# A hybrid RG-LRU and pooling layer on one core: the last norm of a block moved behind the next block's heads, small copies on POOL, split parts first in a head pair

## The reference

```python
proj = rmsnorm(x, norm1_g) @ w_in                  # 1024 -> 4096: x_a | x_b | g_a | g_b
c = causal_conv4(x_a)                              # state: last 3 rows
r, i = sigmoid(c @ w_r + b_r), sigmoid(c @ w_i + b_i)   # 8 heads of 128
a = exp(8 * r * log_sigmoid(lam)); bt = sqrt(1 - a*a) * i * c   # 1 for the root at position 0
h[t] = a[t] * h[t-1] + bt[t]                       # scan over time
d = moving_mean(x_b, windows 2, 4, 8, 16) - x_b    # state: last 15 rows
y_b = grouped(d @ pool_w) * pool_scale
merged = sigmoid(g_a) * (h @ w_br_a) + sigmoid(g_b) * (y_b @ w_br_b)
x = x + merged @ w_out
x = x + (silu(n @ w_g) * (n @ w_u)) @ w_down       # n = rmsnorm(x, norm2_g), hidden 2816
y = rmsnorm(x, final_g)
```

## Time and profile before

| | |
|---|---|
| time, median of 3 runs | 2940.25 us (2940.04 to 2941.14) |
| the profiled execution, its own time | 2941.63 us |
| its span, first to last instruction | 2939.8 us |
| TensorE busy | 2874.5 us (98%) |
| VectorE, ScalarE busy | 1956.4 us (67%), 1263.1 us (43%) |
| POOL busy | 0.2 us, 4 instructions |
| granted clock of TensorE, mean | 0.990 |
| DMA | 354.43 MB, 121 GB/s |

### The profile page before, as it was taken

The page is one execution under the profiler, slowest core; times in us unless marked ns, Lnnn a source line. Parts: engine busy times, 40 slices in busy tenths (PEclk is TensorE's granted clock), DMA queues, the critical chain, the costliest instruction groups (busy, mean ns, idle before and its releaser), DMA issues.

```text
span 2939.8 us, 37519 instructions
## 1 busy us (share of the span) xinstructions
PE 2874.5 (98%) x15006; PEld 2829.8 (96%) x15006; DVE 1956.4 (67%) x2946; ACT 1263.1 (43%) x1745; POOL 0.2 (0%) x4
## 2 busy tenths in 40 slices
PE   8799999999999999999999999999999999999998
PEld 7789999999999999999999999999999999999998
DVE  7657666667576676776666757766667576666656
ACT  4743433347434333483333325833333366343222
POOL 0000000000000000000000000000000000000000
PEclk9999999999999999999999999999999999999999
DMA  4263333333334333333333333334333333333332
GB/s 142 83 219 110 137 122 115 115 108 124 130 118 142 115 108 122 107 117 130 129 130 109 122 115 117 129 115 138 115 115 117 120 110 122 111 107 127 115 117 81
DMA packets 113163, 354.43 MB, mean 121 GB/s; under 512 B 12128, under 2 KB 30816, under 8 KB 112992
## 3 DMA queue, kind: packets, MB, share of 16 engines
q1 hardware_dynamic: 102480, 336.14, 33.2%
q10 hardware_dynamic: 10512, 15.90, 1.6%
HBM read 339.12 MB, written 12.87 MB: 120 GB/s over the span
## 4 chain that ended last, share of the span: by engine, by line
PE 84%; DVE 9%; ACT 3%; issue 2%; DMA 1%; SPq 0%; ACTq 0%; DVEq 0%
PE ps L294 84%; DVE gb L705 2%; DVE wring L827 2%; DVE main L713 1%; DVE ylo L710 1%; DVE tot L660 1%; ACT wring L407 1%; DVE tmp L739 1%; ACT L489 0%; DVE rstd_n L666 0%; DMA fused<-main 0%; PE ps L313 0%; ACT tmp L489 0%; ACT tmp L480 0%; ACT tmp L482 0%
## 5 line engine op out<-in xcount | busy, mean ns | idle before, releaser
L294 PE MATMUL ps<-yhi,wring 128*128 128x416 f32 x4800 | 1312.3, 352 | 1.1 <-DVE wring L827 1.1
L827 DVE TENSOR_TENSOR wring<-wraw,wring 128x1024 fp32r<-128x1024 f32 x610 | 746.2, 1224 | 328.4 <-ACT wring L407 327.0
L294 PE MATMUL ps<-xhi,wring 128*128 128x416 f32 (+1 forms) x3200 | 890.7, 357 | 41.6 <-DVE wring L827 40.3
L294 PEld LDWEIGHTS ps<-yhi,wring 128*128 128x128 f32 x4800 | 900.7, 188 | 10.6 <-issue 1.8
L294 PE MATMUL ps<-ylo,wring 128*128 128x416 f32 x2400 | 841.1, 350 | 0.0
L407 ACT ACTIVATE wring<-wraw 128x1024 fp32r<-128x1024 f32 x610 | 640.9, 1051 | 459.3 <-PE ps L294 438.0
L294 PEld LDWEIGHTS ps<-xhi,wring 128*128 128x128 f32 x3200 | 610.5, 191 | 54.7 <-DVE wring L827 37.7
L294 PE MATMUL ps<-xlo,wring 128*128 128x416 f32 (+1 forms) x1600 | 568.4, 355 | 0.0
L294 PE MATMUL ps<-hhi,wring 128*128 128x416 f32 x1760 | 485.0, 352 | 0.0
L294 PEld LDWEIGHTS ps<-ylo,wring 128*128 128x128 f32 x2400 | 452.2, 188 | 5.1 <-issue 1.4
L294 PEld LDWEIGHTS ps<-hhi,wring 128*128 128x128 f32 x1760 | 329.3, 188 | 2.4
(11 more groups left out here) (108 smaller groups left out, 1520.5 us busy)
## 6 DMA issues: line engine op xcount, KB each, us to landing
wraw<-dwm SPq DMA_DIRECT2D x577, 512.0 KB, 3.2
wraw<-fused SPq DMA_DIRECT2D x40, 512.0 KB, 3.2
dy<-main ACTq DMA_DIRECT2D x36, 208.0 KB, 2.1
xres<-dx ACTq DMA_DIRECT2D x32, 208.0 KB, 3.0
sraw<-dws SPq DMA_DIRECT2D x24, 256.0 KB, 3.8
fused<-main SPq DMA_DIRECT2D x16, 256.0 KB, 7.0
xres<-dx SPq DMA_DIRECT2D x4, 216.0 KB, 5.7
xres<-dx ACTq DMA_DIRECT2D x4, 216.0 KB, 6.0
```

The costliest lines, as they stand in the source:

```text
L294: mm = nc.tensor.matmul(out, wt[:, c * P:(c + 1) * P], x, start=(first and q == 0), stop=(last and q == 2))
L827: V.tensor_tensor(wring[:, n % RING, 1, :], wraw[:, n % RAW, :], wring[:, n % RING, 0, :].bitcast(f32), SUB).then_inc(w_lo, 1)
```

## The change

- The convolution's and the window's small copies between `state` and `tbuf` move from VectorE to a new program of POOL, with waits between them on both sides (`xa_hist`, `xa_saved`, `xb_hist`, `xb_saved`).
- Blocks 1 to 4: `invert` of n3 moves behind head pair 0, `finish` 0 to 3 behind pair 1 and 4 to 7 behind pair 2; the stores stand on ScalarE before pair 2 and before pair 3.
- In a head pair, VectorE's `ahead(b, "ga", 2p)` stands before the squares instead of behind them, and ScalarE's `ahead` for gb before the sigmoids instead of behind the exponentials.
- Block 0: the column sum n1 stands behind xa 2 instead of xa 0. The 16 w products are no longer in one run ahead of the a products: four stand behind each second a product. Their chunks lie in `tmp` instead of `main`, the stores one slot earlier, and VectorE waits for all stores behind the a products, ahead of the windows.
- ScalarE computes one Sqrt of a single column ahead of the last root.

```diff
@@ def pe_order(b):
-        if h == 0 and b == 0:
+        if h == 2 and b == 0:
             out.append(("n1", 0, 0))
...
-    if b == 0:
-        out += [("w", 0, q) for q in range(16)]
-    out += [("a", b, m) for m in range(KT)]
+    for m in range(KT):
+        out.append(("a", b, m))
+        if b == 0 and m % 2:
+            out += [("w", 0, 2 * (m - 1) + q) for q in range(4)]
@@ def chunk(q):
-            return main[:].rearrange("p k c -> p (k c)")[:, 512 * (q % 6):512 * (q % 6) + 512]
+            return tmp[:].rearrange("p k c -> p (k c)")[:, 512 * (q % 6):512 * (q % 6) + 512]
@@ SP
-                    if n == SLOT[("w", 0, 2 * g + 1)] + 5 + RAW:
+                    if n == SLOT[("w", 0, 2 * g + 1)] + 4 + RAW:
                         for q in range(4 * g, 4 * g + 4):
                             save_fused(q)
@@ POOL (new)
+            def conv_history(b, h):
+                if h >= 3:
+                    pool.wait_ge(tap, upto(b, h - 2, 3, 6))
+                elif b:
+                    pool.wait_ge(d_done, b * KT)
+                if b:
+                    pool.wait_ge(xa_saved, upto(b, 0, 1, 2))
+                for o, n, s in conv_parts(b):
+                    copy(tbuf[:, h % 3, o:o + CH], state[:, h, s:s + CH]).then_inc(xa_hist, 1)
+
+            def conv_save(b, h):
+                pool.wait_ge(xa_hist, upto(b, h + 1, 1, 2))
+                if b:
+                    pool.wait_ge(xa_t, upto(b, h + 1, 1, 2) - KT)
+                else:
+                    pool.wait_ge(*drain(("xa", b, h)))
+                for o, n, s in conv_parts(b):
+                    copy(state[:, h, s:s + CH], tbuf[:, h % 3, o + n:o + n + CH]).then_inc(xa_saved, 1)
...
+            for b in range(NB):
+                for h in range(KT + 1):
+                    if h < KT:
+                        conv_history(b, h)
+                    if h:
+                        conv_save(b, h - 1)
...
@@ ScalarE: conv_in(b, h)
                 if h >= 3:
                     act.wait_ge(tap, upto(b, h - 2, 3, 6))
+                    act.wait_ge(xa_saved, upto(b, h - 2, 1, 2))
+                else:
+                    act.wait_ge(xb_saved, upto(b, 0, 1, 2))
@@ ScalarE: heads(b, p)
                 bw = BW[b]
+                if p:
+                    ahead(b, "gb", GBP[p - 1][-1])
                 for j in range(2):
...
-                if p:
-                    ahead(b, "gb", GBP[p - 1][-1])
                 for j in range(2):
                     act.wait_ge(q_done, b * KT + 2 * p + j + 1)
@@ ScalarE: the blocks
-                    if b and h == 6:
-                        for m in range(4):
-                            store_y(b - 1, m)
...
-                    elif b:
-                        for m in range(4, KT):
+                    if b and p >= 2:
+                        for m in range(4 * p - 8, 4 * p - 4):
                             store_y(b - 1, m)
                     heads(b, p)
...
+            A(warm[:], epsc[:], ACT.Sqrt)
             root(("n3", NB - 1, 0), 2)
@@ VectorE: heads(b, p)
                     V.tensor_tensor(tmp[:, 4 * j + 1, 0:bw], tmp[:, 4 * j + 1, 0:bw], gb[:, h, 0:bw], MUL).then_inc(ix_done, 1)
+                ahead(b, "ga", 2 * p)
                 for j in range(2):
...
                     V.scalar_tensor_tensor(tq, tr, 1.0, tq, ADD, MUL).then_inc(q_done, 1)
-                ahead(b, "ga", 2 * p)
@@ VectorE: the blocks
-                    if b and h == 3:
-                        invert(("n3", b - 1, 0), 2)
-                    if b and h >= 4:
-                        finish(b - 1, 2 * h - 8)
-                        finish(b - 1, 2 * h - 7)
...
                     if side_unit(b, p) + 2 < NSIDE:
                         split_side(side_unit(b, p) + 2)
...
+                    if b and p == 0:
+                        invert(("n3", b - 1, 0), 2)
+                    if b and p in (1, 2):
+                        for m in range(4 * p - 4, 4 * p):
+                            finish(b - 1, m)
```

More of the change, by code:

```diff
@@ L125, in side_before @@
     for g in range(4):
[L126 removed]
+        at.setdefault(SLOT[("w", 0, 2 * g + 1)] + 4 + RAW, []).append(g + 8)
     return at
@@ L275, in _, with conv_parts, pool_parts, pool_history @@
             sp.wait_ge(y_stored, 16 * KT * NB)
+        @block.gpsimd
+        def _(pool):
+            copy = nc.gpsimd.tensor_copy
+            def conv_parts(b):
+                return [(0, PT[b], S_CP)] + ([(PT[b] + CH, DEC, S_CS)] if b == SB else [])
+            def pool_parts(b):
+                return [(0, PT[b], S_PP)] + ([(PT[b] + PH, DEC, S_PS)] if b == SB else [])
+            def conv_history(b, h):
[15 more added lines that the diff above has]
+                    copy(state[:, h, s:s + CH], tbuf[:, h % 3, o + n:o + n + CH]).then_inc(xa_saved, 1)
+            def pool_history(b, k):
+                if k >= 3:
+                    pool.wait_ge(d_done, b * KT + k - 2)
+                else:
+                    pool.wait_ge(tap, upto(b + 1, 0, 3, 6))
+                if b:
+                    pool.wait_ge(xb_saved, upto(b, 0, 1, 2))
+                for o, n, s in pool_parts(b):
+                    copy(tbuf[:, k % 3, o:o + PH], state[:, k, s:s + PH]).then_inc(xb_hist, 1)
+            def pool_save(b, k):
+                pool.wait_ge(xb_hist, upto(b, k + 1, 1, 2))
+                pool.wait_ge(*drain(("xb", b, k)))
+                if b == SB:
+                    pool.wait_ge(xb_t, k + 1)
+                for o, n, s in pool_parts(b):
+                    copy(state[:, k, s:s + PH], tbuf[:, k % 3, o + n:o + n + PH]).then_inc(xb_saved, 1)
+            pool.wait_ge(tables_in, 32)
+            for b in range(NB):
[4 more added lines that the diff above has]
+                        conv_save(b, h - 1)
+                for k in range(KT + 1):
+                    if k < KT:
+                        pool_history(b, k)
+                    if k:
+                        pool_save(b, k - 1)
@@ L370, in _ @@
                                                  for k in (5, 6, 7)} | {0: ((ya_hi, n8 + 5), (ya_lo, n8 + 5))} if m == 0 else ())
+                    if b == 0 and m % 2:
+                        fuse(m // 2)
                 for k in range(KT):
@@ L587, in _ @@
                     ahead(b, "gb", k)
-                if b == 0:
-                    for g in range(4):
+                for m in range(KT):
+                    ahead(b, "a", m)
+                    if b == 0 and m % 2:
+                        g = m // 2
                         ahead(0, "w", 2 * g)
@@ L596, in _ @@
                                 act.wait_ge(fused_saved[q % 6], 16 * (q // 6))
+                            else:
+                                act.wait_ge(ya_lo, KT)
                             A(chunk(q), bank(("w", 0, q)), ACT.Copy).then_inc(drained[JOB[("w", 0, q)] % 8], 1)
-                for m in range(KT):
-                    ahead(b, "a", m)
                 for k in range(KT):
@@ L683, in conv @@
                 bw, pt, t = BW[b], PT[b], tbuf[:, h % 3, :]
-                parts = [(0, pt, 0, S_CP)] + ([(pt + CH, DEC, pt, S_CS)] if b == SB else [])
-                for o, n, c, s in parts:
-                    V.tensor_copy(t[:, o:o + CH], state[:, h, s:s + CH]).then_inc(xa_hist, 1)
+                parts = [(0, pt, 0)] + ([(pt + CH, DEC, pt)] if b == SB else [])
                 dve.wait_ge(xa_hist, upto(b, h + 1, 1, 2))
@@ L701, in conv @@
                 for i, v in enumerate((2, 1, 0)):
-                    for q, (o, n, c, s) in enumerate(parts):
+                    for q, (o, n, c) in enumerate(parts):
                         if i:
@@ L920, in _ @@
                     name = ("a", b, m)
-                    if b or m:
-                        ahead(b, "a", m)
+                    ahead(b, "a", m)
                     done(name)
@@ L928, in _ @@
                     V.tensor_tensor(main[:, m, :], bank(name)[:, 0:LW], ga[:, m, :], MUL).then_inc(drained[JOB[name] % 8], 1)
+                    if b == 0 and m % 2:
+                        g = m // 2
+                        ahead(0, "w", 2 * g)
+                        for q in (4 * g + 1, 4 * g + 3):
+                            done(("w", 0, q))
+                            if q >= 6:
+                                dve.wait_ge(fused_saved[q % 6], 16 * (q // 6))
+                            else:
+                                dve.wait_ge(ya_lo, KT)
+                            V.tensor_copy(chunk(q), bank(("w", 0, q))).then_inc(drained[JOB[("w", 0, q)] % 8], 1)
+                        ahead(0, "w", 2 * g + 1)
+                        split_side(6 + g)
+                if b == 0:
+                    for q in range(6):
+                        dve.wait_ge(fused_saved[q], 16 * (3 if q < 4 else 2))
                 for k in range(KT):
```

33 lines of the change are left out of this document (10 added, 23 removed).

## The result

The changed kernel takes 2945.85 us, median of 20 runs (2943.31 to 2948.83); the kernel before, beside it, 2940.97 us, also 20 runs (2939.48 to 2944.21). The ratio is 1.0016, 95% interval [1.001, 1.0022]: between 0.1 and 0.2% slower. The prediction was 2943.4 us, range 2933 to 2951, with a chance of 0.58 for "same", within 0.2%. The profiled execution took 2946.3 us, its span 2944.5, which is 4.7 more than before.

The account below looks back on a forecast made before the run. TensorE, busy 98%, was taken as the bound, with the head-pair chain only just hidden. Block 0 -4.1 us and blocks 1 to 4 +7.3 sum to +3.2 on the median of 2940.25: 2943.4 us, range 2933 to 2951.

Parts of the forecast that it names:

- Stall of ga2 gone, chain as the bound: Blocks 1 to 4: the wait at ga2 goes, the head-pair chain stalls TensorE before "a"; 25.1 us against 27.0.
- The deciding step: Head pairs, blocks 1 to 4: ScalarE's stores wait for finishes ahead of the next sigmoids; block 1 steps 22.1 and 20.7 us.
- rival 1: Blocks 1 to 4: the chain doesn't wait for the stores, no stall is left, 2909 us; chance 0.08.
- Clock: Behind the new gap before "a", blocks 1 to 4: a slow clock costs 2.3 us each, 9.2 in all.
- rival 2: Blocks 1 to 4: the clock stays up after the new gaps, -6.0 us, 2934; chance 0.12.
- Start and small copies: Block 0: start priced 0, VectorE's first convolution 1.7 us later; POOL copies take back 0.27 x 7.
- Block 0 behind the heads: Block 0 from "a" 0 on: "a" 0 4.7 us earlier, xb at 214.0; block 0 in all -4.1 us.
- The wait for the saved products: Block 0, before the windows: VectorE waits about 9 us for the fused save and reaches the windows at 226.8.
- Rival 3: POOL copies and VectorE hold each other up: at 0.5 us a copy, +8.7 us, 2952; chance 0.15.
- Tail: End of the kernel: the early Sqrt brings nothing, 0 us; the root waits 1.13 us for TensorE.

Follow-up runs that it names:

- experiment 1: The changed kernel with all eight stores of y issued by ScalarE behind head pair 3, finishes left in place: 2912.59 us.
- experiment 9: Experiment 8 with the stores of the norm issued from POOL's queue, each behind its own finish: 2904.86 us.
- experiment 10: Experiment 8 with stores 0 to 3 ahead of head pair 3 and 4 to 7 right behind it, still on ScalarE: 2904.7 us.
- experiment 2: The changed kernel with 28 extra matmuls, results overwritten, ahead of the first "a" product in blocks 1 to 4: 2937.91 us.
- experiment 4: The changed kernel with all small copies between state and tbuf back on VectorE and no POOL program: 2948.94 us.
- experiment 7: Experiment 1 with the column sum n1 behind xa 1 instead of xa 2: 2909.15 us.
- experiments 1 to 4: Four runs, each the changed kernel with one edit; the third puts the norm and its stores back in the convolutions: 2925.94 us.
- experiment 8: Experiment 7 with VectorE's lac steps spread over block 0's convolutions and 28 unused matmuls ahead of block 0's first "a" product: 2907.23 us.

## Why the prediction was right

*Stall of ga2 gone, chain as the bound.* Right. In block 1 the first sigmoid is 5.36 us behind the first gate (forecast 5.24), the steps are 16.61, 22.29 and 21.12 (16.6, 22.1, 20.7), and the split of the first "a" weight stands 12.71 behind pair 3 (12.65). The forecast has the two long steps a little too small: after the last finish ScalarE goes on 0.48 and 0.68 us later, not 0.4. The gap before "a" in block 1 is 5.27 (5.4), the small one at gb5 1.05 (0.5). In all, waits took 36.7 - 9.75 = 26.9 us of blocks 1 to 4, forecast 25.1.

*The deciding step*, that the stores and not the finishes hold the chain, is shown by experiments 1, 9 and 10 together; rival 1 (chance 0.08) was wrong about this kernel, and its price of 2909 was nearly that of experiment 1.

*Clock.* 9.75 us by the rows of after, 9.2 by the forecast; experiment 2 gives back 9.4. The value of 2.3 a block, from the three slow products of the earlier trace rows, was the right choice, and zero (rival 2, 2934) wasn't. (Rival 2's case, block 1 of the kernel before, was a stall of 2.64 us by the timeline, not 2.8; the new ones are 4.75 to 5.60.) Blocks 1 to 4 together: 26.9 + 9.75 - 27.2 = +9.5, forecast +7.3. The mis-sized term is the stall, by 1.8.

*Start and small copies.* Forecast at nothing and at a loss of 1.7 taken back by 1.9. Measured one by one they are larger: POOL's copies bring 4.1 us (experiment 4), n1 behind a later product costs block 0 time: moved one product forward it gives some 1.4 us (experiment 7). The convolutions of block 0 run every 5.52 us, forecast 5.5, before 5.79. That the two roughly offset each other was right, though how nearly they did was in part luck, since both were larger than forecast. The split that releases "a" 0 came at 153.31 (152.1). VectorE's first convolution came 2.6 us later than before (29.04 to 31.60), not 1.7, behind this row of VectorE, after; in experiments 1 to 4, which start in the same way, the reciprocal stands at 25.64 to 26.84, so at least part of this is scatter:

```profile
26.97 2.85 DVE L732 RECIPROCAL rstd_n<-rstd_n 128x432 f32<-128x432 f32 x1 [2.84 <-ACT rstd_n L497]
```

*Block 0 behind the heads.* "a" 0 to the first xb product took 59.70 us (58.1 + 2.3 forecast), xb started at 214.28 (214.0). The wait for the saved products was there, and smaller than forecast (7.2, not 9 us), so VectorE was back at the windows at 224.95 and not 226.8, and the 0.8 us that TensorE was to lose at "b" is missing:

```profile
224.95 1.22 DVE L890 TENSOR_TENSOR wring<-wraw,wring 128x1024 fp32r<-128x1024 f32 x1 [7.16 <-DMA fused<-tmp]
```

That makes -4.7, forecast -4.1: "a" 0 came 1.2 us later than forecast, and the stages behind it gave more than that back.

*Rival 3.* The two engines do get in each other's way, but the one that pays is POOL. SBUF — State Buffer (Trainium skill), "SBUF: two separate sides", says whoever comes first keeps the shared port for its whole instruction. The trace agrees in one direction. Of POOL's 192 copies, 113 start while VectorE is at work, and 101 of these take over 0.3 us, up to 1.62; the other 79 take 0.19. In the other direction it does not: 45 times VectorE starts an instruction within a copy that came first, and that instruction is 0.005 us longer in the mean, 0.028 at most, than the same one in experiment 4, where POOL has no copies. The measurement decides: these copies held VectorE up by nothing that counts. Its splits took 1224 ns in the mean before and 1223 after.

*Tail.* Forecast zero. The table load of the early Sqrt now runs at 2931.82, but the root waits for TensorE all the same, 0.78 us (1.13 in the earlier trace rows):

```profile
2931.82 1.28 ACT L706 ACT_TABLE_LOAD   x1
...
2934.10 0.61 ACT L497 ACTIVATE rstd_n<-ps,epsc 128x416 f32<-128x416 f32 x1 [0.78 <-PE ps L374]
```

*The sum.* -4.7 + 9.5 is +4.8, the spans say +4.7, the medians +4.9; forecast +3.2. What stays open is why the runs of one kernel scatter by some 5 us, of which the profile of a single execution tells little.

## What to carry to other kernels

Before work is moved off a busy engine, list what each queue holds *behind* the instructions that wait for it: a DMA issue that waits for its data stops every computation behind it on that engine. Put it behind work that is surely done, or on a queue with nothing urgent (33 us here). A stall that goes shows up again at the next door of the same late chain, so price the chain, not the wait; and count a long gap of TensorE twice, as the gap and as the slow clock behind it.

## What the runs showed of the hardware that I had not expected

- The slow clock behind a gap of 4.75 to 5.60 us costs 2.0 to 2.8 us, in all four blocks, and 28 matmuls of no use in the gap take nearly all of it back (27.91 to 18.47 us).
- Eight stores of 208 KB issued in a row hold ScalarE's queue for 4.26 us in block 1 of experiment 1 and 5.44 us in experiment 8, 0.53 to 0.68 us each. Four issued in step with VectorE's finishes, one every 0.56 us, take as long as the finishes: 2.28 us on POOL's queue (some 0.54 an issue, experiment 9), 2.03 on ScalarE's (some 0.34 an issue, changed kernel). They land in 3.2 us (median) from POOL, in 3.8 from ScalarE; in experiment 10, still from ScalarE, in 2.2.
- POOL's tiny copies are the side that yields: 0.31 to 0.54 us in the mean of a line, against 0.19 for three columns undisturbed. VectorE's instructions beside them keep their length.
